# Row writes for the second rotation, and a re-ordered way from the last projection to the first expert step

## What is computed

```python
def _rotate(x, ang):
    x1, x2 = jnp.split(x, 2, axis=-1)
    cos, sin = jnp.cos(ang)[None, :, None, :], jnp.sin(ang)[None, :, None, :]
    return jnp.concatenate([x1 * cos - x2 * sin, x1 * sin + x2 * cos], axis=-1)

def rope_2d_2(x, row, col):              # heads of 64: 32 turned by the row, 32 by the column
    half = x.shape[-1] // 2
    xr, xc = x[..., :half], x[..., half:]
    return jnp.concatenate([_rotate(xr, _axis_angles(row, half)),
                            _rotate(xc, _axis_angles(col, half))], axis=-1)

def expert_choice_ffn(h, w_router, w_gate, w_up, w_down):     # 16 experts, 64 tokens each
    aff = jax.nn.softmax(jnp.einsum('bnd,de->bne', h, w_router), axis=-1)
    top_w, top_idx = lax.top_k(jnp.swapaxes(aff, 1, 2), cap)  # cap = 64
    xe = jax.vmap(lambda hb, ib: hb[ib])(h, top_idx)
    g = jnp.einsum('becd,edf->becf', xe, w_gate)
    u = jnp.einsum('becd,edf->becf', xe, w_up)
    y = jnp.einsum('becf,efd->becd', jax.nn.silu(g) * u, w_down) * top_w[..., None]
    return scatter_add(top_idx, y)

# second block: h = modulate(rmsnorm(x)); q, k, v and gates = h @ w_in; q and k rotated;
# windowed attention and a gated mix; x += g1 * (merged @ w_out); h2 = modulate(rmsnorm(x));
# x += g2 * expert_choice_ffn(h2, ...); out = rmsnorm(x)
```

## Time and profile before

| | us |
|---|---|
| runs of the kernel before, median (lowest to highest) | 2479.23 (2478.89 to 2479.68) |
| the profiled execution, its own time | 2479.24 |
| its span, first to last instruction | 2477.0 |
| TensorE busy | 2310.4 (93%) |
| VectorE busy | 892.9 (36%) |
| ScalarE busy | 619.6 (25%) |
| GpSimd busy | 147.0 (6%) |
| mean granted TensorE clock | 0.978 |

### The profile page before, as it was taken

How to read it: one execution, slowest core, us unless ns; L and a number is a source line. 1 busy time by engine, 2 the same in 40 slices (tenths; PEclk the granted TensorE clock), 3 DMA queues, 4 the chain that set the end, 5 groups by cost and what they waited for, 6 DMA issues and landing times.

```text
span 2477.0 us, 25779 instructions
## 1 busy us (share of the span) xinstructions
PE 2310.4 (93%) x11168; PEld 1507.6 (61%) x11168; DVE 892.9 (36%) x1171; ACT 619.6 (25%) x877; POOL 147.0 (6%) x140
## 2 busy tenths in 40 slices
PE   6999999999999999998999997998988899898998
PEld 4874878877888878886667886434343434343433
DVE  4937445555678334544632433010101010000001
ACT  5214333243334226315542221000000000000001
POOL 0221000110000011210000020000000000000000
PEclk9999999999999999999999998999999999999999
DMA  7220444344555332210002234999999999999997
GB/s 272 102 80 1 151 151 155 106 166 155 177 181 201 129 136 76 77 69 35 1 26 81 98 136 177 417 428 428 427 428 428 427 427 428 427 429 427 428 427 291
DMA packets 113062, 570.10 MB, mean 230 GB/s; under 512 B 5598, under 2 KB 28423, under 8 KB 87863
## 3 DMA queue, kind: packets, MB, share of 16 engines
q1 hardware_dynamic: 97072, 523.57, 52.3%
q0 software_dynamic: 7152, 27.99, 3.2%
q10 hardware_dynamic: 8727, 16.91, 2.0%
HBM read 566.35 MB, written 2.10 MB: 229 GB/s over the span
## 4 chain that ended last, share of the span: by engine, by line
PE 73%; DMA 20%; DVE 4%; ACT 2%; issue 1%; SPq 0%; ACTq 0%; POOL 0%; DVEq 0%; POOLq 0%
PE ps L793 42%; PE ps L1322 8%; DMA arena<-in_w_exp_up 8%; PE ps L1416 6%; DMA arena<-in_w_exp_gate 5%; DMA weights<-in_w_exp_gate 3%; PE ps L1305 3%; PE ps L1208 1%; PE ps L1226 1%; DMA weights<-in_w_exp_up 1%; DMA weights<-in_w_exp_down 1%; PE ps L1166 1%; DMA weights<-in_w_up 1%; PE ps L1032 1%; PE ps L1337 1%
## 5 line engine op out<-in xcount | busy, mean ns | idle before, releaser
L793 PE MATMUL ps<-weights_r 128*128 128x512 f32 (+1 forms) x2784 | 859.7, 388 | 12.4 <-DVE hT_r L1995 4.0
L793 PEld LDWEIGHTS ps<-weights_r 128*128 128x128 f32 x2784 | 520.8, 189 | 125.4 <-issue 18.7
L793 PE MATMUL ps<-hT_r,weights_r 128*128 128x512 f32 x1264 | 461.8, 390 | 0.0
L1322 PE MATMUL ps<-weights,arena 128*64 128x512 f32 x768 | 353.4, 617 | 60.4 <-DMA weights<-in_w_exp_up 46.5
L1324 PE MATMUL ps<-weights,arena 128*64 128x512 f32 x768 | 354.1, 618 | 0.0
L1322 PEld LDWEIGHTS ps<-weights,arena 128*64 128x64 f32 x768 | 105.9, 142 | 288.7 <-issue 286.6
L1976 DVE TENSOR_TENSOR weights_r<-weights,weights_r 128x4096 fp32r<-128x4096 f32 (+1 forms) x46 | 197.1, 4284 | 210.7 <-ACT weights_r L1501 208.9
L793 PEld LDWEIGHTS ps<-hT_r,weights_r 128*128 128x128 f32 x1264 | 237.8, 188 | 50.7 <-issue 2.2
L793 PE MATMUL ps<-arena_r,weights_r 128*128 128x512 f32 (+1 forms) x640 | 225.6, 388 | 0.0
L1501 ACT ACTIVATE weights_r<-weights 128x4096 fp32r<-128x4096 f32 (+1 forms) x46 | 161.7, 3514 | 215.2 <-PE ps L793 118.8
L2588 DVE TENSOR_TENSOR hT<-hT,ps 128x512 f32<-128x512 f32 x32 | 22.0, 688 | 460.8 <-PE ps L1324 460.8
(11 more groups left out here) (306 smaller groups left out, 2445.0 us busy)
## 6 DMA issues: line engine op xcount, KB each, us to landing
weights<-in_w_exp_gate SPq DMA_DIRECT2D x48, 2048.0 KB, 23.1
weights<-in_w_exp_up SPq DMA_DIRECT2D x48, 2048.0 KB, 27.0
weights<-in_w_exp_down SPq DMA_DIRECT2D x42, 2048.0 KB, 27.1
weights<-in_w_in SPq DMA_DIRECT2D x18, 2048.0 KB, 8.3
arena<-in_w_exp_gate SPq DMA_DIRECT2D x16, 2048.0 KB, 27.5
arena<-in_w_exp_up SPq DMA_DIRECT2D x16, 2048.0 KB, 27.7
arena<-in_w_exp_down SPq DMA_DIRECT2D x14, 2048.0 KB, 28.5
weights<-in_w_up SPq DMA_DIRECT2D x22, 1024.0 KB, 7.9
```

Of the source, the lines that this page charges most:

```text
L793: last = pe.matmul(t, a if w_first else b, b if w_first else a, start=(k == 0 and n == 0), stop=(k == kt - 1 and n == len(pairs) - 1))
L1322: la = pe.matmul(bank(b0 + n)[0:64, :], xe[:, 2 * j + r, 0:64], wa[:, r, n * 512:(n + 1) * 512], start=start, stop=stop)
```

## The change

Two edits are joined.

The second rotation uses the way of the first. The columns of queries and keys in `w_in_2` are laid out anew before the launch (`halves_of_heads`), so that the two halves of a rotated pair stand in the halves of a head, the same for queries and keys; the scores are sums over a head and do not see the order. The ten swap products, their PSUM tiles and the matrix `swap2` go, and one table `rope` serves both blocks.

The way from the last projection on is re-ordered. Router steps 3 to 6 are each done earlier, step 6 in the middle of the last tile; the exponential stands before the first token copies; the first maximum reads the affinities in PSUM, and ScalarE copies them out later; the ranks are turned unmasked, beside the turned `chosen`, and masked at the copy. The first pair's gather is cut into columns 0 to 1 before the first step, 2 to 3 inside step 0 and 4 to 7 inside step 1. The eight pieces of the first up steps are loaded in halves, each when the half step before it has freed its place.

```diff
-            roped("q2", ("in2", 4), 0, 4, "swap2", raw2)
-            roped("q2", ("in2", 5), 4, 4, "swap2", raw2, first=lambda: swap("q2", 3, "swap2", raw2))
-            swap("q2", 7, "swap2", raw2)
-            roped("k2", ("in2", 6), 0, 2, "swap2", raw2)
-            swap("k2", 1, "swap2", raw2)
+            for nq in range(2):
+                feature_tiles(("in2", 4 + nq), [("q2", 4 * nq + i) for i in range(4)], h_parts)
+            feature_tiles(("in2", 6), [("k2", i) for i in range(2)], h_parts)
...
-            def rope_halves(i, dst):
+            def rope_halves(tag, i, g, cs, rawbuf, rsinbuf, rcosbuf, dst):
...
+                    last = ve.tensor_tensor(rsinbuf[q:q + 32, i % 2, :], rawbuf[o:o + 32, i % 2, :],
+                                            cs[o:o + 32, 1, :], ALU.mult)
...
-                rope_sum("q2", i, 8 + i, rope_cs2, rsin2, rcos2, q2[:, i, :])
+                rope_halves("q2", i, 8 + i, rope_cs2, raw2, rsin2, rcos2, q2[:, i, :])
...
+                    feature_tiles((tag, 1), [(tag, n)], x, c0=n % 4 * P,
+                                  between=(lambda: route_step(6)) if (tag, n) == ("out2", 7) else None)
-                    for k in {4: (0, 1, 2), 5: (3,), 6: (4,), 7: (5,)}[n]:
+                    for k in {4: (0, 1, 2, 3), 5: (4,), 6: (5,), 7: ()}[n]:
...
-            for k in range(6, KT):
-                route_step(k)
-                norm_step(6, "n4", L, k)
+            norm_step(6, "n4", L, 6)
+            route_step(7)
+            norm_step(6, "n4", L, 7)
...
-            keep_tokens(0, 0)
             act_e.wait_ge(S["row_ready"], 1)
             A(aff[:, :, :], aff[:, :, :], ACT.Exp).then_inc(S["aff_exp"], 1)
+            keep_tokens(0, 0)
+            keep_tokens(0, 1)
+            act_e.wait_ge(S["aff_read"], 1)
+            free("affT", "A", A(aff_t[0:NE, :], wait_full(act_e, "affT")[0:NE, :], ACT.Copy))
...
-            free("affT", "D", ve.tensor_copy(aff_t[0:NE, :], wait_full(ve, "affT")[0:NE, :]))
-            wait_freed(ve, "affT")
-            src = aff_t[0:NE, :]
+            src = wait_full(ve, "affT")[0:NE, :]
...
-            ve.tensor_tensor(rank[0:NE, :], rank[0:NE, :], chosen[0:NE, :], ALU.mult).then_inc(S["rank_ready"], 1)
-            free("slotT", "D", ve.tensor_copy(slot_of[:, :, :].rearrange("p a b -> p (a b)"),
-                                              wait_full(ve, "slotT")[:, 0:TT * NE]))
+            free("slotT", "D", ve.tensor_tensor(slot_of[:, :, :].rearrange("p a b -> p (a b)"),
+                                                wait_full(ve, "slotT")[:, 0:TT * NE],
+                                                chosen_tok.rearrange("p t e -> p (t e)"), ALU.mult))
...
             select(0)
+            ve.wait_ge(S["rank_ready"], 1)
+            ve.tensor_tensor(rank[0:NE, :], rank[0:NE, :], chosen[0:NE, :], ALU.mult).then_inc(S["rank_masked"], 1)
...
+            pe.wait_ge(S["chosen_ready"], 1)
+            a = claim(pe, "chosenT")
+            for t in range(TT):
+                last = pe.transpose(a[:, t * NE:(t + 1) * NE], chosen[0:NE, t * P:(t + 1) * P], ident[0:NE, 0:NE])
+            fill("chosenT", last)
...
-            gather(0, range(2))
+            gather(0, range(1))
...
+                    if it == 0 and first == 0 and r == 0:
+                        la.then_inc(S["half_free"], 1)
+                        lb.then_inc(S["half_free"], 1)
+                        if j < 2:
+                            gather(0, (range(1, 2), range(2, STEPS))[j])
...
+            for j in range(STEPS):
+                for r in range(2):
+                    if r == 0:
+                        sp.wait_ge(S["half_free"], 2 * j + 2)
+                    else:
+                        sp.wait_ge(S["chunk_free"], LOOP_FREE + 2 * j + 2)
+                    for e in range(2):
+                        src = w_exp_up_2[0, e, 256 * j:256 * j + 256, :].rearrange("(p r) n -> p r n", r=2)
+                        sp.dma_start(eslots[2 * j + e][:, r * DE:(r + 1) * DE], src[:, r, :]).then_inc(
+                            S[f"landed{2 * j + e}"], 16)
```

More of the change, by code:

```diff
@@ L244, in plan_banks @@
         b.add(("mix", g), "D")
[L245 to L250, removed]
+    for i in range(8):
+        b.add(("q2", i), "A")
+    for i in range(2):
+        b.add(("k2", i), "A")
     for t in range(TT):
@@ L267, in plan_banks @@
         if t == 0:
-            b.add("affT", "D")
+            b.add("affT", "A")
     b.add("perm", "A")
+    b.add("chosenT", "A")
     b.add("slotT", "D")
@@ L803, in feature_tiles @@
                         last = product(t, w, src, k, kt, (c0 + n * P, c0 + n * P + P), (0, width), True)
+                        if between and k == kt // 2:
+                            between()
                     fill(tn, last)
@@ L898, in mod_step @@
                 fill((tag, c), last)
[L900 to L908, removed]
-                    if i > i0 or first is not None:
-                        if i > i0:
-                            swap(tag, i - 1, matrix, rawbuf)
-                        else:
-                            first()
             def merge(tag):
@@ L1309, in gather @@
                             last.then_inc(S["xe_full"], 1)
+                        elif it == 0 and d == 1:
+                            last.then_inc(S["xe_first"], 1)
             def widen(it, j, first, full):
-                if first == 0 and j == 0:
+                if it == 0 and first == 0 and j == 0:
+                    pe.wait_ge(S["xe_first_kept"], 1)
+                if first == 0 and j == (it == 0):
                     pe.wait_ge(S["xe_low"], it + 1)
@@ L1915, in keep_gathered @@
                              bias=perm_cols[:, 1, r, j:j + 1], scale=perm_cols[:, 0, r, j:j + 1])
+                    if it == 0 and d == 1:
+                        last.then_inc(S["xe_first_kept"], 1)
                 last.then_inc(S["xe_low"], 1)
@@ L2210, in _ @@
             for i in range(4):
-                rope_halves(i, obuf[:, 2 + 2 * i, :])
+                rope_halves("qk1", i, i, rope_cs, raw, rsin, rcos, obuf[:, 2 + 2 * i, :])
             prepare(("in1", 1))
@@ L2743, in shape_constants @@
     put("ident", p == n)
-    def swap(half):
-        m = np.zeros((P, P), f)
-        for i in range(P):
-            if i % (2 * half) < half:
-                m[i + half, i] = -1.0
-            else:
-                m[i - half, i] = 1.0
-        return m
-    put("swap2", swap(16))
     mask = np.zeros((P, 2, P), f)
@@ L2774, in shape_constants @@
     a1 = np.tile(a1, (4, 1)).astype(np.float64)
-    a2 = np.concatenate([np.tile(row[None] * inv[:, None], (2, 1)), np.tile(col[None] * inv[:, None], (2, 1))], 0)
-    a2 = np.tile(a2, (2, 1)).astype(np.float64)
     r1 = rope_table(a1, np.where(np.arange(P) % 64 < 32, 1.0, -1.0)).astype(f)
-    r2 = rope_table(a2, np.ones(P)).astype(f)
     k = np.arange(L)
@@ L2799, with halves_of_heads @@
         "w_exp_gate_2", "w_exp_up_2", "w_exp_down_2", "final_g_2"]
+def halves_of_heads(w):
+    q = w[:, :, 2 * D:2 * D + (NH + NKV) * HD].reshape(1, D, NH + NKV, 2, 2, HD // 4)
+    w = w.copy()
+    w[:, :, 2 * D:2 * D + (NH + NKV) * HD] = q.swapaxes(3, 4).reshape(1, D, (NH + NKV) * HD)
+    return w
 def kernel(**inputs):
```

81 lines of the change are left out of this document (40 added, 41 removed).

## The result

The changed kernel takes 2462.01 us (median of five runs, 2461.3 to 2469.71) against 2479.68 for the kernel before beside it: a ratio of 0.9934, 95% interval 0.9917 to 0.9951. The profiled execution took 2461.99 us with a span of 2459.7, so 17.25 us less than the profiled one of before. Taken again on another occasion (*changed_again*) the same kernel gave 2464.3 and a ratio of 0.9936 (0.9922 to 0.9949).

The account below looks back on a forecast made before the run. It took TensorE's chain ahead of the expert-weight stream, then that stream at 427 GB/s, as the bound. Rotation 8.9, constants 0.2 and the way to the stream 7.5 make 16.6 us: 2479.2 to 2462.6 us, range 2459.5 to 2469.5.

Parts of the forecast that it names:

- Rotation, 8.9 + 0.2: Second block's projections: dropping ten swap products from TensorE's path saves 8.9 us; the smaller constants save 0.2 us.
- VectorE's cover, "some 15 us": Behind the second rotation: key copies end at 1095.5, attention wants them at about 1110, so VectorE's lag costs nothing.
- Last tile later by 2.1: Last projection: two more router steps ahead of its last tile's end delay five of the first eight loads, at no cost.
- Selection, 1.7 of router steps and 2.0 out of the chain: Last projection to gather: 1.69 us of router steps moved ahead of the last tile; three pieces leaving selection save 2.0 us.
- The dip behind tile 4: Last projection: half clock after the router steps cost tile 5 1.6 us; four steps add 0.4, bounds -1.6 and +1.6.
- Gather and first half step: 6.9 less forecast: Gather to first freed slot: gather and copies 4.2 us instead of 8.3, half step 3.5 plus 0.8 for low clock.
- the same delay: First expert step: clock rises 5.8 us after the gather begins, as before, so 1.6 us run at half speed, losing 0.8.
- The hole, about 6 us: Expert-weight stream: DMA idle between the first eight pieces and the first load into a freed slot, 16.6 us before.
- Holes and rate of the halves, 0.4 + 0.6 lost: Expert-weight stream: holes of 1.7 us instead of 1.3 lose 0.4; 1 MB loads at 421 GB/s against 427 lose 0.6.
- The clock takes more or less: Tile 5 and first half step: more low clock, 2466.5 us (chance 0.20); no dip or half speed, 2459.8 (0.10).
- The other rivals: Slow halves 2465.8 us (0.07); VectorE bounding rotation 2471.5 (0.05); change without effect 2475 (0.04); half-clock steps 2492.6 (0.03).

Follow-up runs that it names:

- rot_only: Kernel before with only the second rotation changed (swap products replaced by row writes, columns re-laid): 2465.58 us, ratio 0.9949.
- products_back: Changed kernel with one unread product of a swap's size put ahead of each of the ten second-rotation tiles: 2472.05 us, ratio 0.9968.
- two_steps_clock_kept: Changed kernel with unread products in TensorE's pauses, first gathered column used at once, router steps 2, 2, 1, 1 behind tiles 4 to 7: 2456.89 us, ratio 0.9907.
- rows_twice: Changed kernel with every row write of the second rotation done twice on VectorE: 2487.99 us, ratio 1.0033.
- chain_only: Kernel before with only the re-ordered way from the last projection on, rotation unchanged: 2474.2 us, ratio 0.9970.
- steps_back: Changed kernel with router steps as before (3, 1, 1, 1 behind tiles 4 to 7, two behind the last): 2458.3 us, ratio 0.9913.
- whole_pieces: Changed kernel with the first up pieces loaded whole (2 MB) behind a whole step instead of in halves: 2470.82 us, ratio 0.9966.

## Why the prediction was right

2462.6 was forecast and 2462.01 measured. Between the two profiles the 17.25 us are 9.24 (rotation) + 1.54 (two falls of the clock in before, one in after) - 1.25 (B) + 6.68 (M to H) + 1.04 (H to the end). The mechanism is right in its two parts. That the total agrees to 0.6 us is luck: the first step gained 1.8 less than forecast, and the stream, which was to lose 1.0, came out 1.04 shorter. Step by step:

- *Rotation, 8.9 + 0.2.* Measured 9.24 in the chain, by *rot_only* the same, and by *products_back* 9.0 for the ten products alone (7.8 to 10.0 by the medians). The other 1.54 between B and M is the net of three falls of the clock: before has one at the start of attention and one in the merge, after has one in the mix. Whether the swap products have a part in it is open. All three kernels with ten such products have a fall in the merge, and of the ten without them two have it (*changed_again*, *two_steps_clock_kept*); so the products are not needed for it, but they may make it likelier. The forecast had no term for this. The 0.2 for the constants can't be told apart from the scatter of B.
- *VectorE's cover, "some 15 us": wrong, without effect.* It was 4 us in the profile after and 5 by *rows_twice*. I took attention's wait for the keys as the end, and forgot 3.5 us of context copies on VectorE behind them (a wait only for the last work of the queue), and 3.9 us of low parts; and each row write takes 0.91 us, not 0.87. The forecast also let both key tiles end "near 1092" when by its own 1085 and 4.3 us a tile they end at 1093.6. Spread over ten tiles the 4 to 5 us are 0.4 to 0.5 us: at 4.8 us a tile instead of 4.3 it would have been gone.
- *Last tile later by 2.1.* From M to the end of the last tile 55.21 us against 53.32: 1.9.
- *Selection, 1.7 of router steps and 2.0 out of the chain.* From that tile to the gather 22.44 against 25.94 us: 3.5, where 3.7 were forecast.
- *The dip behind tile 4.* I added 0.4 to the 1.6 of before. It fell as deep as before (7.22 against 7.19), so nothing was added. But it is the four steps that make it sure: 8 of 8 profiles with four have it, 1 of 4 with three, none of 1 with two. The profile of before was the odd one. Against an execution of before without that fall the move would cost 1.6 us.
- *Gather and first half step: 6.9 less forecast, 5.07 measured* (15.39 to 10.32 us from the gather's start to H). The gather's 16 records took 3.77 us for 3.3; the first half took 5.60 for 4.3, since the clock rose 4.1 us into the step (1527.8 against its start at 1523.72) and not 1.6 us into it (1534.4 against 1532.8). This is the term that was mis-sized, and the step in it that fails is "the same delay": the delay of the clock's rise behind the gather's start is not constant. From the gather's start to H it is 10.32 us in after and 10.18 in *rows_twice*, but 8.29 to 8.38 in *changed_again*, *chain_only*, *products_back* and *steps_back*, where 8.5 was forecast. With M to H of 86.75 on the mean of the five kernels that have the change's chain whole, the gain is 7.9, and 8.5 was forecast.
- *The hole, about 6 us.* 8.4, by the same 2 us.
- *Holes and rate of the halves, 0.4 + 0.6 lost.* *whole_pieces* has 1.0 less from H to the end. Against the profile of before, though, the stretch is 1.04 shorter, not longer. That profile has 933.64 there, 2 us more than the two other kernels that load whole pieces (931.36, 931.63). These 2 us make up for the 1.8 that the first step cost. They arise in the last load that the chain waits for; behind its landing all take 30.3 us. In before, *rot_only* and *whole_pieces*:

```profile
2421.87 27.08 DMA weights<-in_w_exp_down
2406.59 27.01 DMA weights<-in_w_exp_down
2411.28 27.74 DMA weights<-in_w_exp_down
```

It lands 903.35, 901.05 and 901.34 us after H. *steps_back* has the same late landing (903.68, against 902.27 in after). Why it lands late in some executions I can't say.
- *The clock takes more or less*, 0.20 and 0.10: both happened, a little, in the two profiles of the changed kernel. The other rivals (slow halves, VectorE, a change without effect, steps at half clock one after another) did not; the mean clock was 0.98 from 1560 on and the stream ran at 427 GB/s. (The 880 us from 1560 to 2440 are 36% of the span, not 38%; nothing hangs on it.)

The Trainium skill (DMA: Bandwidth & Descriptors, section Bandwidth) gives 341 GB/s for a transfer of 1 MB, measured on transfers issued from GpSimd. Here SyncE issues them, and queued one behind the other they moved 421 GB/s, and *whole_pieces* shows that they cost 1 us in all.

## What to carry to other kernels

When work is moved onto an engine that lags behind, count all that stands in its queue up to the wait that ends last, not only the moved work's own reader; 15 us of cover were 5. When a chain with pauses of TensorE ends in a stage of products, look at the granted clock in it: here unread products in the pauses, an earlier first column, and one narrow step fewer in a row gave 4 to 6 us between M and H (7 to 10 by the medians), beside the 7 to 9 us of the re-ordered chain itself. A change is read best between marks in the trace that lie on the path, because the profile's own time carries several falls of the clock that come and go between executions of one kernel.

## What the hardware did that I had not expected

*Falls of the clock wander.* A stretch of products with the same instructions has a fall of the granted clock to half in some executions and not in others. One costs 1.5 to 1.6 us: the merge's second long piece is 88.9 us with it and 87.3 without, the mix 8.8 to 9.0 with it and 7.41 without. From B to M seven profiles with the new rotation lie within 0.2 us (415.25 to 415.41) and have one fall each, and two with three and four falls are 3.2 and 4.7 longer. That is of the size of the spread of the runs (2461.3 to 2469.71); that it is all of it was not shown.

*Narrow products behind each other bring one.* Four router steps, 32 records in 3.5 us, were followed by a fall in each of eight profiles; three (24 records in 2.6 us) in one of four.

*A busy TensorE can be a faster one.* Nine and more products that nobody reads made the gather behind them 1.2 us shorter, and 1.65 where the clock was up throughout (2.12 us for 3.77, in the other three kernels). The first half step was at full clock in all four kernels with them; without them it was so in four of seven with the re-ordered chain, and else took 2.0 us more. What they cost in the first of the four: the last four at a clock of 0.58, 2.00 us.

*A row write depends on its neighbour.* 32x512 took 0.91 us on the mean. For the eight query tiles, where GpSimd makes its product of the same raw tile meanwhile, four writes took 3.8 us (the first four 4.75); for the two key tiles, where it had finished, 2.77; and so did the second set in *rows_twice*. That GpSimd is the reason rests on this coincidence in time; no run took its product away.

Open: why the clock falls in the mix, at the start of attention or in the merge in some executions and whether the swap products have a part in it, why that last load lands 2 us later in some, and whether a smaller dose of unread products behind the turn of the ranks would keep the clock without delaying the gather.
